# Set-up of a decoder step: x transposed a chunk ahead of its product in a ring of seven banks, parameter rows behind chunk 0 and from two queues

## What is computed

```python
def rmsnorm(x, g):
    y = x * lax.rsqrt(jnp.mean(x * x, axis=-1, keepdims=True) + EPS)
    return y * g

def swiglu(x, g, w_in, w_out):
    gate, up = jnp.split(rmsnorm(x, g) @ w_in, 2, axis=-1)
    return (jax.nn.silu(gate) * up) @ w_out

x = x + 0.5 * swiglu(x, norm_ffn1_g, w_ffn1_in, w_ffn1_out)   # D = 1024, D_FF = 2816
...
h = rmsnorm(x, norm_mix_g)         # then w_in, three branches, merge
...
x = x + 0.5 * swiglu(x, norm_ffn2_g, w_ffn2_in, w_ffn2_out)
```

## Time and profile before

| what | value |
|---|---|
| median of 3 runs | 3393.15 us (3388.55 to 3401.1) |
| profiled execution | 3391.9 us |
| its span | 3390.3 us |
| mean granted clock of TensorE | 0.964 of full speed |
| PE busy | 3204.7 us, 95% of the span |
| DVE busy | 1719.2 us, 51% |
| ACT busy | 891.9 us, 26% |
| POOL busy | 667.4 us, 20% |
| DMA | 265.48 MB, mean 78 GB/s |

### The profile page before, as it was taken

One profiled execution on the slowest core, in us unless ns is written; L12 is line 12 of the kernel. 1 busy time (PEld: TensorE's weight loads), 2 busy tenths in 40 slices (PEclk: granted clock), 3 DMA queues, 4 the chain that ended last, 5 costly groups with the idle time before them and its releaser, 6 DMA issues. The chain is left out here.

```text
span 3390.3 us, 51925 instructions
## 1 busy us (share of the span) xinstructions
PE 3204.7 (95%) x19826; PEld 2955.5 (87%) x19826; DVE 1719.2 (51%) x3013; ACT 891.9 (26%) x1604; POOL 667.4 (20%) x415
## 2 busy tenths in 40 slices
PE   6999999999998999999779898998999999999999
PEld 6999999999898999899545555567999999999999
DVE  5333333334589999996234444444744333333333
ACT  4111111112332332433333333332132111111111
POOL 1211212213533312233320000001221112111111
PEclk8999999999999999999779999998999999999999
DMA  3111111112222223122543445433431111111111
GB/s 97 50 43 37 49 43 43 43 43 67 72 79 75 86 68 87 39 84 84 168 161 113 130 135 165 133 110 117 136 110 51 45 42 49 44 43 43 43 37 66
DMA packets 253376, 265.48 MB, mean 78 GB/s; under 512 B 14527, under 2 KB 193314, under 8 KB 253214
## 3 DMA queue, kind: packets, MB, share of 16 engines
q1 hardware_dynamic: 247854, 254.64, 24.0%
q0 software_dynamic: 4128, 4.20, 0.4%
q10 hardware_dynamic: 1232, 4.46, 0.4%
HBM read 226.20 MB, written 37.05 MB: 78 GB/s over the span
## 5 line engine op out<-in xcount | busy, mean ns | idle before, releaser
L331 PE MATMUL bank<-h_hi,w_hi 128*128 128x362 f32 (+1 forms) x3384 | 1125.8, 333 | 37.4 <-DVE h_lo L218 19.0
L331 PE MATMUL bank<-h_lo,w_hi 128*128 128x362 f32 (+1 forms) x3384 | 1119.1, 331 | 0.0
L331 PE MATMUL bank<-h_hi,w_lo 128*128 128x362 f32 (+1 forms) x3384 | 1115.6, 330 | 0.0
L331 PEld LDWEIGHTS bank<-h_hi,w_hi 128*128 128x128 f32 x3384 | 643.3, 190 | 44.8 <-issue 24.9
L331 PEld LDWEIGHTS bank<-h_lo,w_hi 128*128 128x128 f32 x3384 | 643.7, 190 | 2.8
L331 PEld LDWEIGHTS bank<-h_hi,w_lo 128*128 128x128 f32 x3384 | 644.3, 190 | 0.0
L388 POOL TENSOR_TENSOR w_lo<-raw,w_hi 128x1024 fp32r<-128x1024 f32 x132 | 316.1, 2402 | 1291.3 <-ACT w_hi L483 1291.3
L550 DVE SCALAR_TENSOR_TENSOR x<-bank,x 128x362 f32<-128x362 f32 (+1 forms) x528 | 280.3, 534 | 213.6 <-PE bank L331 213.6
L331 PE MATMUL bank<-a_hi_ffn,w_hi 128*128 128x362 f32 (+1 forms) x1056 | 348.9, 330 | 4.3 <-DVE x L550 2.7
L331 PE MATMUL bank<-a_lo_ffn,w_hi 128*128 128x362 f32 (+1 forms) x1056 | 347.1, 329 | 0.0
L331 PE MATMUL bank<-a_hi_ffn,w_lo 128*128 128x362 f32 (+1 forms) x1056 | 345.7, 327 | 0.0
(11 more groups left out here) (357 smaller groups left out, 4161.0 us busy)
## 6 DMA issues: line engine op xcount, KB each, us to landing
raw<-in_w_ffn_in SPq DMA_DIRECT2D x88, 512.0 KB, 3.8
k_ring<-in_cache_k SPq DMA_DIRECT2D x128, 256.0 KB, 3.8
v_ring<-in_cache_v SPq DMA_DIRECT2D x128, 256.0 KB, 4.0
raw<-in_w_in SPq DMA_DIRECT2D x53, 512.0 KB, 4.9
raw<-in_w_ffn_out SPq DMA_DIRECT2D x44, 512.0 KB, 3.5
kept_g<-stage SPq DMA_DIRECT2D x24, 544.0 KB, 3.1
gate<-kept_g SPq DMA_DIRECT2D x24, 544.0 KB, 3.6
x<-x_kept SPq DMA_DIRECT2D x8, 544.0 KB, 4.4
```

Of the source, the lines that this page charges most:

```text
L331: mm = pe.matmul(out, left, right, start=(start and i == 0 and j == 0), stop=(stop and i == n - 1 and j == 2))
```

## The change

It has three parts, all in `setup_and_feed`.

1. The parameters' job moves from place 0 to place 6, behind the six x jobs of chunk 0. PE's first wait is now for the first x tile, and for the identity matrix.
2. Row loads 5 to 12 of `params` (conv_w to state_h) are issued by ACT, behind the third x tile and ahead of the fourth. SP keeps the other eight row loads, and then starts on the weight units.
3. The ring grows from five to seven banks, in the order 3, 4, 5, 6, 7, 1, 2, and PE turns a chunk ahead: jobs 0 to 12 before chunk 0's product, jobs 13 to 18 before chunk 1's and none before chunk 2's. A wait of ACT that a later one covers is dropped.

The numbers of the last job of each chunk, who copies which job, and all sizes stay.

```diff
--- before.py
+++ after.py
@@ -724,8 +724,7 @@
         ("ba", 4, "lru_ba", "(k c) -> k c"), ("bi", 4, "lru_bi", "(k c) -> k c"),
         ("lam", 4, "lru_lambda", "(k c) -> k c"), ("gmq", 1, "mem_q_norm_g", None),
         ("gmk", 1, "mem_k_norm_g", None), ("h0", 32, "state_h", "b (k c) -> (b k) c"))]
-    jobs = [dict(src=[prow[:, :]], dst=par[:, :], psum=lambda b: b[:, 0:N_ROWS],
-                 needs=[(made, 3), (rows_loaded, 16 * (len(params) + 4))])]
+    jobs = []
     for t, (t0, w) in enumerate(TT):
         for half in range(2):
             jobs.append(dict(
@@ -733,13 +732,17 @@
                 dst=x[:, 4 * half:4 * half + 4, t0:t0 + w],
                 psum=lambda b, w=w: b[:, 0:4 * w].rearrange("p (q n) -> p q n", q=4),
                 needs=[(x_loaded[t], 16)]))
+    jobs[0]["needs"].append((made, 3))
+
+    jobs.insert(6, dict(src=[prow[:, :]], dst=par[:, :], psum=lambda b: b[:, 0:N_ROWS],
+                        needs=[(rows_loaded, 16 * (len(params) + 4))]))
 
     norm = feed.norm
-    RING = 5
+    RING = 7
 
     def slot(n):
 
-        return bank[3 + n % RING]
+        return bank[(3, 4, 5, 6, 7, 1, 2)[n % RING]]
 
     def turn(pe, n):
         job = jobs[n]
@@ -761,9 +764,12 @@
 
     last_job = (6, 12, 18)
 
+    def some_params(queue, first, last):
+        for r, n, src in params[first:last]:
+            queue.dma_start(prow[r:r + n, :], src).then_inc(rows_loaded, 16)
+
     def on_sp(sp):
-        for r, n, src in params:
-            sp.dma_start(prow[r:r + n, :], src).then_inc(rows_loaded, 16)
+        some_params(sp, 0, 4)
         for name, key in (("gq", "q_norm_g"), ("gk", "k_norm_g")):
             for half in range(2):
                 sp.dma_start(prow[ROWS[name]:ROWS[name] + 1, half * DH:(half + 1) * DH],
@@ -800,7 +806,7 @@
 
     def before(pe, u, c):
         if u == 0:
-            for n in range(0 if c == 0 else last_job[c - 1] + 1, last_job[c] + 1):
+            for n in (range(0, 13), range(13, 19), ())[c]:
                 turn(pe, n)
         elif c == 0:
             pe.wait_ge(evicted[0], 10)
@@ -809,12 +815,12 @@
     def on_act(act):
         for t, (t0, w) in enumerate(TT):
             act.dma_start(xin[0:w, t, :], x_rows[t] if t < 8 else s_rows).then_inc(x_loaded[t], 16)
+            if t == 2:
+                some_params(act, 4, len(params))
         for c in range(len(CH)):
             for n in range(0 if c == 0 else last_job[c - 1] + 2, last_job[c] + 1, 2):
                 evict(act, act.copy, n)
             feed.high_part(act, 0, c, c == 0)
-            if c == 0:
-                act.wait_ge(evicted[0], 1)
             act.wait_ge(evicted[0], last_job[c] // 2 + 1)
             act.wait_ge(evicted[1], last_job[c] // 2)
             norm.act_high(act, c)
```

## The result

| what | before | after |
|---|---|---|
| median of 7 runs each, taken together | 3388.55 us (3380.78 to 3401.1) | 3363.89 us (3352.93 to 3372.11) |
| ratio after / before, 95% interval | | 0.9931 (0.9909 to 0.9952) |
| profiled execution | 3391.9 us | 3366.95 us |
| mean granted clock of TensorE | 0.964 | 0.969 |
| PE busy | 3204.7 us | 3188.4 us |

Twice more beside the kernel before, the same kernel gave 0.9963 (0.9947 to 0.9979) and 0.9953 (0.9936 to 0.9969); the three ratios, weighted by their intervals, make 0.9952, about 16 us.

What follows compares the result with a forecast made beforehand. The set-up was taken to be bound by the chain behind chunk 2's h_hi and squares, not PE. 13.5 + 1.1 - 0.6 = 14.0 us off 3391.9 gives 3377.9; with 1.25 us for the median, 3379 us, range 3371 to 3388.

Steps and rivals of the forecast that it cites:

- Part 2: Set-up DMA: eight row loads on ACT let unit 0 land at 16.0 instead of 17.0, gain 1.0 us.
- Part 1: Set-up start: parameters turned behind chunk 0's x; gains nothing alone, since unit 0's load still lands at 16.99.
- Part 3: Set-up chunks: turning ahead puts chunk 2's h_hi at 31.9 against 45.44, 13.5 us earlier including 1.0 from Part 2.
- the third reciprocal: Chain behind the squares: its 1.13 us wait for PE's last sum behind unit 1 goes, gain 1.1 us.
- wait for sg: PE before unit 2: its wait for the first scaled gate grows from 5.8 to over 7 us.
- The clock at unit 2's start: TensorE at unit 2: a longer wait keeps the clock low for longer, 0.6 us lost, between nothing and 1.4.
- Rival B: Set-up DMA: ACT's row loads hold x back, unit 0 lands by 12; gain 18 us, 3375; chance 0.15.
- Rival A: Set-up DMA: the engines were the bound, unit 0 still lands at 17.0; gain 13.0 us, 3380; chance 0.15.
- C: Set-up: TensorE becomes the bound if its clock stays low; gain 4 us, 3389; chance 0.11.
- D: Chunk 0's product: late tiles 3 to 5 delay it, a loss if it starts at 34; slower, 3411; chance 0.04.
- What was to show it wrong: Set-up: cast before 14 or after 18, DVE copies over 0.8 us, third reciprocal waiting, or span off by over 3 us.
- The second sign: Whole span: differing from the set-up's gain by over 3 us would mean something later had moved.

Runs made afterwards that it cites:

- e9: Kernel before with ACT issuing eight row loads, parameters still turned first and ring still five; ratio 1.0006, unit 2 at 72.87 us.
- e3: Changed kernel with all 16 row loads on SP again; ratio 0.9961, unit 2 at 61.11 us.
- e5: Changed kernel with a ring of five and each chunk turned in front of its own product; ratio 0.9987, unit 2 at 66.72 us.
- e1: Kernel before measured again, nothing edited; ratio 1.0000, unit 2 at 72.75 us.
- e7: Changed kernel with ACT's eight row loads issued by GpSimd; unit 0's load went out at 8.3 us; ratio 0.9974, unit 2 at 61.37 us.
- e11: Changed kernel with GpSimd issuing ACT's eight rows, semaphore raised first, and x tile 3 waiting for tile 0's landing; ratio 0.9959, unit 2 at 56.91 us.
- e4: Changed kernel with ACT's eight row loads behind all nine x loads; ratio 0.9966, unit 2 at 62.55 us.
- e8: Changed kernel with rows on GpSimd and ACT issuing x tiles 3 to 8 only once unit 0 landed; ratio 0.9967, unit 2 at 60.45 us.

## Why the prediction was wrong

The forecast was 3379 us, the measurement 3363.89. Of the 15.1 us between them:

- **4.6 us are the base.** The median of the three runs shown was 3393.15, and of all seven of the kernel before it was 3388.55. The forecast was a gain of 14 us from the former.
- **4.7 us are one term of Part 2,** and this is the step that failed: unit 0's landing, "I take 16.0, a gain of 1.0 us, near the upper end, since the row of 12 to 13 us, with both queues full, is the one that resembles the case". It landed at 10.2 and its cast ran at 11.45. I took the equal packets of two full queues from the stretch behind 12 us and laid it over the stretch from 7 us on. But there it moved 44 packets and SP's 613: its first three tiles were nearly through, and its fourth had been issued behind the unit. The line for it was in my own text, "on ACT the same eight push x's tiles 3 to 8 back by about 3 us"; I priced it as 0.5 MB that goes at an eighth of the rate, instead of asking who has work in each microsecond. Everything behind the cast moved with it: unit 2 at 55.5 for 60.2.
- **The rest, 5.8 us, came behind the set-up and is about what the attention stage scatters with its granted clock.** The first profiles differ there by 6.1 us, two profiles of one program by 15. With all three measurements the gain is 16 us (0.9952), against 16.4 to 18.8 at x_kept. I had allowed medians to differ by 3 or 4 us on their own; that was too little for a lower end of 3371.

By the steps of the prediction:

- **Part 1** was to give nothing alone, which no run shows, for none has it alone. But part 2 gives at most 2 us without it (e9), which the sum of single terms didn't say: the three parts together move unit 2 by 17 to 19 us, 1 and 3 by 12 to 14 (e3), 1 and 2 by 6 to 8 (e5), part 2 by 0 to 2.
- **Part 3 was right in the main.** The distances of 8.4 and 6.5 us hold to 0.1 us in the first execution of the changed kernel and in e3. In the other two the second is 7.0 and 6.7: PE ends the turns of the late tiles 3 to 5 at 18.3 and 18.0 there, not at 17.1, its turns for chunk 2 start at 22.1 and 21.8 instead of 20.9, and ACT waits for the copies. So PE, which the prediction had off the path, costs up to 0.5 us. Else it came as worked out: DVE's copies are undisturbed under w_lo; the third reciprocal no longer waits. Its worth against the kernel before was read from an execution with slow chunk 0 products, and is 10 to 11 us (e1, e5) where these run faster. PE's waits came out nearly as described: one for h_lo of 2.4 us before chunk 2, where I had 1.5. The one ahead of chunk 0's product is missing, since PE is still turning tile 3 to 5 from 12.51 to 17.09, which land late. Its wait for sg was 6.05, 8.0 and 7.7 us in three executions, where I had over 7.
- **The clock at unit 2's start**, 0.6 us lost, was priced by a longer wait. The runs don't bear that out: the changed kernel's shortest wait (6.05) was followed by the lowest clock, 0.83 in the first 15.16 us, and the waits of 8.0 and 7.7 by 0.90, where the kernel before had 0.89 and 0.90 behind 5.8. From unit 2 to x_kept it took 753.5, 752.8 and 752.7 us, the kernel before 752.5 and 752.7, so the term is 0 to 1.
- **Rival B** had the size (18 us; measured 17 to 19) and the place (the unit in by 12, h_hi near 13), and 0.15 was too low a chance for it. Its wording, "ACT's row loads hold x back", is half right: not their data (e7) but the 3 us in which ACT issues them and no x tile (e11). My words against it, "nothing in the rows holds data back behind them", were true and beside the point.
- **Rival A** is what happens when the rows stand behind x (e4). **C** fell: the reciprocals stand without a gap, and PE still waits 6 us for sg. **D** didn't come: chunk 0's product started at 16.84, not at the 34 that it needed. (Its 3411 should be 3410: 3393 + 17.)
- **What was to show it wrong** did: the cast came before 14, and the spans differ from the set-up's gain by 5.6 us (24.95 less 19.4). The second sign was read as "something later has moved"; it is mainly the scatter of the attention stage and its clock, and the repeated profiles were needed to see it.

What stays open is why x stands still so long, that is, what gives the engines to the load that was issued first. Tile 3 was issued at 5.55, 1.6 us behind the unit, and until 10 us its queue moved next to nothing; in e4 it was the unit, issued at 3.99 behind x tiles, that moved nothing until 8. It looks as if the loads of both queues came to the DMA engines in the order in which they were issued, and shared them only where both are in line. It isn't strict order: in the kernel before, the unit was issued behind all of x and yet shared the engines from 11 to 12 us (86 packets to x's 88), while x went on until 15.9. No run here shows the stage in which they would be put in order.

## What to carry to other kernels

When an edit moves DMA issues between queues, write down for each microsecond which queue has issued what and what is through, before applying a rate: here 3 us passed without an x load being issued, the unit's load was issued in them, and it landed in 6.2 us instead of 14.1. The order of issues across engines can be set deliberately, and e4 against the changed kernel shows what that is worth: 6.8 us of a set-up, for the place of eight small loads. Where a stage's length scatters by 15 us between executions of one program, judge an edit of the first 75 us by a marker behind it, not by the total.

## What the runs showed of the hardware that I had not expected

- **Two queues that both have loads issued don't always share evenly.** With both moving, 12 to 13 us before the change, packets are equal in number, 92 and 93, and the bytes are 7 to 1 for x. This is also how the Trainium skill describes it ("DMA: Bandwidth & Descriptors", section "Queues, rings and completion order": each engine takes a packet from one queue and then from the next), and the trace agrees there. But from 7 to 8 us it is 613 packets to 44 in the changed kernel and 10 to 114 in e4, for the same loads issued in another order.
- **The same load's time to landing goes from 4.0 to 14.1 us with what was issued around it.** The 0.52 MB unit took 4.0 us alone (e8), 6.2 and 7.0 behind three x tiles (after, e11), 10.0 issued behind all of x in the kernel before, and 14.1 issued at 3.99 into a full row of x loads (e4).
- **The same program, the same stage, 15 us apart.** The granted clock of the attention stage was 0.90 and 0.92 in two executions of the kernel before, with equal work; its length was 736.8 and 721.5 us. In the set-up, too, the clock moved the kernel before: chunk 0's products took 6.75 us at granted 0.56 in one profile and 5.38 us at 0.73 in the other, chunk 1's ran at 0.59 and 0.70, and unit 2 started at 74.84 and 72.75.
